# Gate products of the two mixer blocks: two 128-column tiles at a time, as seven half-size block products

## The chip, the cores and the metric

One core of one Trainium2 chip runs the whole program. The metric is the device time of one execution in microseconds, as the median of several runs; less is better. All tensors are float32.

## What is computed

Two blocks of a diffusion-style mixer with expert layers, then one block of a causal mixer. Only the merge of three branches in the first two blocks is touched. Cut to that:

```python
p = h @ w_in[l]          # h: tokens x 1024
g_a, g_b, g_c = jnp.split(jax.nn.sigmoid(p[..., OFF_GATE:]), 3, axis=-1)   # 3 x 1024 wide
merged = g_a * (o_a @ w_branch[0]) + g_b * (o_b @ w_branch[1]) + g_c * (o_c @ w_branch[2])
x = x + gt1 * (merged @ w_out)
```

In the first block (l = 0) there are 768 tokens (512 of x, 256 of the context), in the second (l = 1) 512.

## The kernel before, in words

Activations lie feature-major: `h3[:, k, t]` is feature k*128 + partition of token t, for 8 tiles k. `PLAN[l]` is a list of jobs; every engine walks through the same list in order and does its own part of each job, so the list sets the order of work on all engines (`plan_layer`, L433; the engine programs from L935, L1567, L1645, L1755 on). Two things follow from this: an engine that waits in one job holds back all its later jobs, and what stands in a queue is seen from the list alone.

The part around the change is the dense stage, `conv + gates[2] + gates[0] + gates[1]` (L438 to L440). First come four products `conv_b`, then for each branch (2, 0, 1) and each of eight output tiles d a job `gate` and a job `branch`:

- PE, `gate` (L1083, `product` at L1004): 8 matmuls over k of a 128x128 weight block with all tokens, each split into columns 0 to 511 and 512 to 767 where there are 768 tokens. `branch`: the same with 4 values of k. Each float32 matmul is two instructions in the trace, so a `gate` is 32 instructions in the first block and 16 in the second.
- ScalarE, `gate` (L1906): the sigmoid of the product, PSUM to one of two rows of `probT`.
- VectorE, `branch` (L2287 to L2298): the gate times the branch's product, into `merged`; for branches 0 and 1 a second instruction adds it.

In the first block only, `with_modulation` (L376) spreads 40 jobs `acc` over this list. Each is four VectorE instructions over 1,024 columns that add a 1 MB piece of `w_ada` to running sums in SBUF (L2157, L2159). After four `acc` come the jobs `rsum` (L1134; PE, then a copy on ScalarE) and `adag` (L1143; PE, then VectorE), which turn a finished group into modulation values.

Weights come in chunks through a ring of six SBUF places of 1 MB. A chunk of gate weights is 1024x256, two output tiles. The SP queue issues the loads in the order in which the jobs first need the chunks, and `load` (L1569) waits, before each, until the place's former chunk was used up (`chunk_end`). Since the queue is in order, a load also waits for all loads ahead of it. A chunk of `w_ada` is used up when VectorE has finished its `acc`.

PSUM has eight banks of 512 columns. `begin` (L959) hands three places of two banks each out in turn to the jobs; two single banks, HEAD_SUMS and SIDE, stand beside them. A helper, `Engine.do` (L1725), issues an instruction on VectorE or ScalarE and waits for its end.

## Time and profile before

| what | value |
|---|---|
| median of 3 runs | 3112.27 us |
| lowest, highest | 3110.53, 3115.92 us |
| the profiled execution: its time | 3114.2 us |
| the profiled execution: span, first to last instruction | 3112.4 us |
| mean granted TensorE clock in it | 0.994 |

All durations below come from the profiled execution. Its time stands 1.8 us over its span and 1.9 us over the median of the runs. The page has one row for each engine (busy time), a chain of the work that ended last, and groups of instructions by line. The line numbers are those of the kernel above.

### The profile page before, as it was taken

Reading aid. Unit: us, or ns where it says so; the run is one execution under the profiler, and the core shown is the slowest. Engines: PE = TensorE matmul, PEld = TensorE weight load, DVE = VectorE, ACT = ScalarE, POOL = GpSimd, SP = SyncE. Lnnn points to the kernel's source line nnn. Section 1 sums busy time; section 2 is a strip of 40 time slices with the busy share of each in tenths; the row PEclk is TensorE's granted clock in tenths of the full one; section 3 lists DMA queues with packets and bytes.
Section 4 is the critical chain, followed back from the end, with each engine's and each line's share of the span. In section 5 each row is a group of like instructions: output and inputs, shape, how many; then the busy total and the mean of one; then the engine's idle time right before and its main releaser. Section 6 shows DMA issues by size and latency. Waiting matters only on the chain.

```text
span 3112.4 us, 32607 instructions
## 1 busy us (share of the span) xinstructions
PE 2984.3 (96%) x13043; PEld 1404.1 (45%) x13043; DVE 1052.1 (34%) x1566; ACT 613.1 (20%) x1121; POOL 75.0 (2%) x88
## 2 busy tenths in 40 slices
PE   7999999999999999999999999999979898899999
PEld 4565655555545222222335655444433222234547
DVE  4764645556514000000147554011121010137352
ACT  3135530000003010111031453000011101021161
POOL 1000000000000010101000000000000000000000
PEclk9999999999999999999999999999999999999999
DMA  8120013434413999999870201222489999963200
GB/s 251 41 82 14 15 55 128 176 135 157 161 41 140 397 351 380 355 371 380 298 200 1 68 21 46 68 81 95 162 333 408 408 408 407 408 221 81 68 1 28
DMA packets 266076, 578.83 MB, mean 186 GB/s; under 512 B 62040, under 2 KB 140136, under 8 KB 265800
## 3 DMA queue, kind: packets, MB, share of 16 engines
q1 hardware_dynamic: 258064, 554.09, 48.8%
q0 software_dynamic: 7552, 22.61, 2.4%
q8 instruction: 106, 1.74, 0.2%
q14 instruction: 42, 0.34, 0.0%
q10 hardware_dynamic: 312, 0.05, 0.0%
HBM read 561.49 MB, written 15.20 MB: 185 GB/s over the span
## 4 chain that ended last, share of the span: by engine, by line
PE 84%; DMA 11%; DVE 3%; issue 1%; ACT 1%; SPq 0%; DVEq 0%; POOL 0%; ACTq 0%; POOLq 0%
PE ps L1016 31%; PE ps L1420 9%; PE ps L1535 6%; PE ps L1032 5%; PE ps L1432 5%; PE ps L1080 5%; PE ps L1248 3%; PE ps L1260 3%; PE ps L1294 3%; DMA ring<-in_w_e_up 3%; PE ps L1093 2%; DMA ring<-in_w_e_down 2%; DMA ring<-in_w_e_gate 2%; PE ps L1056 2%; PE ps L1476 2%; PE ps L1230 1%
## 5 line engine op out<-in xcount | busy, mean ns | idle before, releaser
L1016 PE MATMUL ps<-hT,ring 128*128 128x512 f32 (+1 forms) x2080 | 773.2, 529 | 3.0 <-ACT hT L1761 2.9
L1016 PEld LDWEIGHTS ps<-hT,ring 128*128 128x128 f32 x2080 | 394.9, 191 | 367.6 <-issue 343.7
L1420 PE MATMUL ps<-ring,hT 128*64 128x512 f32 x1392 | 333.1, 607 | 17.2 <-DMA ring<-in_w_e_up 11.9
L1420 PEld LDWEIGHTS ps<-ring,hT 128*64 128x64 f32 x1392 | 89.7, 137 | 220.1 <-issue 219.3
L1032 PE MATMUL ps<-hT,ring 128*128 128x512 f32 (+1 forms) x448 | 181.5, 533 | 0.7 <-DVEq L1746 0.7
L1761 ACT ACTIVATE prob<-ps 128x512 f32<-128x512 f32 (+1 forms) x67 | 46.4, 693 | 681.0 <-PE ps L1016 681.0
L1432 PE MATMUL ps<-ring,hT 128*32 128x512 f32 x1392 | 167.4, 598 | 0.5 <-ACT hT L1761 0.5
L1535 PE MATMUL ps<-ring,hT 128*64 128x512 f32 x640 | 150.4, 603 | 15.0 <-DMA ring<-in_w_e_down 10.8
L1761 ACT ACTIVATE prob<-prob,nms 128x768 f32<-128x768 f32 (+5 forms) x224 | 159.2, 711 | 18.9 <-DVE nms L2384 8.6
L1080 PE MATMUL ps<-merged,ring 128*128 128x512 f32 (+1 forms) x384 | 142.7, 526 | 3.1 <-issue 3.1
L1016 PE MATMUL ps<-obuf,ring 128*128 128x512 f32 (+1 forms) x384 | 143.4, 523 | 0.0
L1260 PE MATMUL ps<-con,prob 128*128 128x128 f32 x872 | 140.2, 283 | 1.3 <-DVE merged L2408 0.5
L1260 PEld LDWEIGHTS ps<-con,prob 128*128 128x128 f32 x872 | 96.4, 140 | 89.5 <-issue 78.8
L2534 DVE TENSOR_TENSOR qbuf<-qbuf,ps 128x1536 f32<-128x1536 f32 x8 | 14.0, 1754 | 341.1 <-ACT qbuf L1761 341.1
L1761 ACT ACTIVATE hT<-ps,mod,amp 128x256 f32<-128x256 f32 (+1 forms) x96 | 50.7, 528 | 327.7 <-PE ps L1470 182.1
L2596 DVE SCALAR_TENSOR_TENSOR xT<-ps,mod,xT 128x512 f32<-128x512 f32 x40 | 30.0, 751 | 249.2 <-PE ps L1476 248.8
L1925 ACT COPY merged<-ps 128x512 f32<-128x512 f32 (+1 forms) x128 | 71.5, 559 | 169.9 <-PE ps L1260 129.9
L2296 DVE TENSOR_TENSOR prob<-prob,ps 128x768 f32<-128x768 f32 (+1 forms) x32 | 26.2, 820 | 231.6 <-PE ps L1016 231.6
L1248 PE MATMUL ps<-kbuf,obuf 64*128 64x256 f32 (+2 forms) x576 | 100.9, 464 | 2.5 <-DVEq L1746 2.2
L1080 PEld LDWEIGHTS ps<-merged,ring 128*128 128x128 f32 x384 | 71.2, 190 | 70.5 <-issue 67.4
L1016 PEld LDWEIGHTS ps<-obuf,ring 128*128 128x128 f32 x384 | 72.4, 190 | 66.2 <-issue 63.3
L1294 PE MATMUL ps<-merged,vbuf 128*64 128x256 f32 x736 | 96.7, 390 | 0.9 <-DVE merged L2408 0.9
(333 smaller groups left out, 3029.0 us busy)
## 6 DMA issues: line engine op xcount, KB each, us to landing
ring<-in_w_e_gate SPq DMA_DIRECT2D x95, 1024.0 KB, 12.3
ring<-in_w_e_up SPq DMA_DIRECT2D x83, 1024.0 KB, 9.7
ring<-in_w_e_down SPq DMA_DIRECT2D x76, 1024.0 KB, 9.4
ring<-in_w_in SPq DMA_DIRECT2D x49, 1024.0 KB, 5.3
ring<-in_w_ada SPq DMA_DIRECT2D x48, 1024.0 KB, 7.3
ring<-in_w_e_down SPq DMA_DIRECT2D x32, 512.0 KB, 7.2
ring<-in_w_in SPq DMA_DIRECT2D x48, 256.0 KB, 4.7
merged<-in_w_e_up SPq DMA_DIRECT2D x12, 1024.0 KB, 15.1
```

What stands on the lines that cost most here:

```text
L1016: mm = pe.matmul(ps[:, b + a:b + e], lhs[:, k, :], rhs[:, k, a:e], start=k == 0, stop=k == nk - 1)
L1032: mm = pe.matmul(ps[:, BANK[SIDE]:BANK[SIDE] + hi - lo], ring3(slot)[:, k, m % 2 * P:(m % 2 + 1) * P], h3[:, k, lo:hi], start=k == 0, stop ...
L1056: mm = pe.matmul(ps[:, b:b + CH], o2[:, k, t * P:(t + 1) * P], ring3(slot)[:, k, :], start=k == 0, stop=k == KD - 1)
L1080: mm = pe.matmul(ps[:, b:b + e - a], w[:, k, :], m3[:, k, a:e], start=k == 0, stop=k == KD - 1)
L1248: mm = pe.matmul(ps[:, b[a] + c0:b[a] + c0 + w], q[r, u["g"], u["q0"]:u["q0"] + P], k[r, u["kj"], k0:k0 + w], start=True, stop=True)
L1260: mm = pe.transpose(ps[:, o:o + P], scored(j[1], j[2], a, u)[:, m * P:(m + 1) * P], ident)
L1294: mm = pe.matmul(out_, v(tiles[m], col), exp_, start=m == 0, stop=m == len(tiles) - 1, tile_position=(0, a * HD))
L1420: mm = pe.matmul(ps[e * CX:(e + 1) * CX, b + h * 512:b + (h + 1) * 512], lhs, second_weights(slot_of[sub], e, h), start=k == 0, stop=k == ...
L1432: mm = pe.matmul(ps[q:q + CC, b + 1024:b + 1536], lhs, second_weights(slot_of[k % 2], e, h), start=k == 0, stop=k == KD - 1, tile_position ...
L1535: mm = pe.matmul(to, lhs[:, k, s0:s0 + CX], second_weights(slot, e, h), start=k == 0, stop=k == KD - 1, tile_position=(0, e * CX))
L1761: return sc.activation(o, i, f, **kw)
L1925: A.do(sc.copy(*turned_to(j)), tb_done[r], j)
```

## The change

Two output tiles (256 columns of gate weights, one chunk) become one job `gate2`. The weights are seen as 2x2 blocks (two halves of k, two output tiles), the tokens as 2x2 blocks (two halves of k, two halves of the token columns). Instead of eight block products it makes seven, of 4 values of k with half of the tokens each (384 columns in the first block, 256 in the second), from sums of blocks:

- `hsum`, once in a block, on VectorE: seven instructions that make sums of token blocks. In the first block they lie in ring places 4 and 5, so that the chunks of the dense stage go round the four others.
- `wsum`, once for each pair of tiles, on GpSimd: four instructions of 512 columns that make sums of weight blocks, in one set of buffers. It waits for the chunk and for the last product of the pair before.
- `gate2` on PE: p1; then, after `wsum`, p6 and p5; p7 waits for VectorE's u2, p2 for ScalarE's copy of p1, p4 for u3, p3 for "22". ScalarE copies p1 and takes four sigmoids; VectorE makes five additions. Six of the seven products are thus behind the weight sums.
- The list becomes `gate2`, `branch` 2n, `wsum` of the next pair, `branch` 2n+1. An `acc` stands only behind a `gate2` or an even `branch`; the 12 pairs have 1, 3, 2, 2, 3, 2, 2, 3, 2, 2, 3 and 0 of them behind `gate2` and one each (the last none) behind the even `branch`.

```diff
+        spare = ring[:, RING - 2:RING, :].rearrange("p s f -> p (s f)")
+
+        def four(cols):
+            return cols.rearrange("p (k t) -> p k t", k=4)
+
+        token_sums = [(four(spare[:, 0:2 * NT]), four(spare[:, 2 * NT:4 * NT]),
+                       [spare[:, 4 * NT + k * NT // 2:4 * NT + (k + 1) * NT // 2] for k in range(2)] + [rs[:, 0:NT // 2], rs[:, NT // 2:NT]]),
+                      (h3[:, 0:4, NX:NT], h3[:, 4:8, NX:NT], [m3[:, k, NX:NT] for k in range(4)])]
+        weight_sums = [four(b) for b in (kbuf[:, D:D + 512], vbuf[:, 2 * D:2 * D + 512], pr[:].rearrange("p k t -> p (k t)")[:, D:D + 512])]
...
+            def long(j):
+                return {"hsum": 0, "wsum": 0, "gate2": 2}.get(j[0], 1)
...
-            count, passed, share = len(todo), 0, len(jobs) - 4
+            count, passed, share = len(todo), 0, sum(map(long, jobs)) - 4
             order, due = [], []
             for j in jobs:
                 order.append(j)
-                passed += 1
+                passed += long(j)
                 while due and due[0][0] <= passed:
                     order.append(due.pop(0)[1])
+                if j[0] == "wsum" or j[0] == "branch" and j[3] % 2:
+                    continue
                 while todo and (count - len(todo)) * share < passed * count:
...
-            gates = {br: [(w, l, br, d) for d in range(KD) for w in ("gate", "branch")] for br in range(3)}
-            dense = conv + gates[2] + gates[0] + gates[1]
+            pairs = [(l, br, n) for br in (2, 0, 1) for n in range(KD // 2)]
+            dense = conv + [("hsum", l), ("wsum",) + pairs[0]]
+            for at, (_, br, n) in enumerate(pairs):
+                dense += [("gate2", l, br, n), ("branch", l, br, 2 * n)]
+                dense += [("wsum",) + p for p in pairs[at + 1:at + 2]] + [("branch", l, br, 2 * n + 1)]
...
+                if j == ("hsum", 0):
+                    few[0] = True
+                elif few[0] and j[0] == "wout":
+                    few[0] = False
+                    after_sums.extend((len(chunks), s) for s in (RING - 2, RING - 1))
                 for key in chunk_keys(j):
                     if key not in chunk_key:
-                        add_chunk(key, chunk_dmas(key))
+                        if few[0]:
+                            add_chunk(key, chunk_dmas(key), few[1] % (RING - 2))
+                            few[1] += 1
+                        else:
+                            add_chunk(key, chunk_dmas(key))
...
+            def seven_products(j):
+                l = j[1]
+                half = (NT, NX)[l] // 2
+                cn, slot = weights(chunk_of(j)[0])
+                if j[1:] == PAIRS_FIRST[l]:
+                    need(oT_ready, ("O", l, 2 * TILES[l] - 1))
+                    need(token_sums_ready, ("hsum", l))
+                a = begin(j)
+                b = a + 512
+                third = (HEAD_SUMS, SIDE)[j[3] % 2]
+                c = begin(j + ("c",), third)
+                w = ring3(slot)
+                s1, s2, s4 = weight_sums
+                t1, t2, t4 = token_sums[l]
+                def times(name, bank, lhs, rhs, first):
+                    for k in range(4):
+                        mm = pe.matmul(ps[:, bank:bank + half], lhs[:, k, :], rhs[k] if name == "p4" else rhs[:, k, :],
+                                       start=first and k == 0, stop=k == 3, skip_group_check=not first)
+                    mm.then_inc(seven_full.sem, 1)
+                times("p1", a, w[:, 0:4, 0:P], h3[:, 0:4, 0:half], True)
+                need(weight_sums_ready, ("wsum",) + j[1:])
+                times("p6", b, s2, t2, True)
+                times("p5", c, s1, t1, True)
+                need(seven_added, j[1:] + ("u2",))
+                times("p7", b, w[:, 0:4, P:2 * P], h3[:, 0:4, half:2 * half], False)
+                need(first_product, j[1:])
+                times("p2", a, w[:, 4:8, 0:P], h3[:, 4:8, 0:half], False)
+                need(seven_added, j[1:] + ("u3",))
+                times("p4", b, w[:, 4:8, P:2 * P], t4, False)
+                need(seven_added, j[1:] + ("22",))
+                times("p3", c, s4, h3[:, 4:8, half:2 * half], False)
+                chunk_end[cn] = (seven_full.sem, seven_full.at[j[1:] + ("p3",)])
...
+                for since, place in after_sums:
+                    if n >= since and slot == place and (chunk_prev[n] is None or chunk_prev[n] < since):
+                        sp.wait_ge(seven_full.sem, seven_full.at[LAST_PAIR[0] + ("p3",)])
...
+            def weight_sum(j):
+                slot, value = chunk_at[chunk_key[chunk_of(j)[0]]]
+                pool.wait_ge(w_full[slot], value)
+                if ("gate2",) + j[1:] in gate_before:
+                    pool.wait_ge(seven_full.sem, seven_full.at[gate_before[("gate2",) + j[1:]] + ("p3",)])
+                else:
+                    pool.wait_ge(token_sums_ready.sem, token_sums_ready.at["hsum", j[1]])
+                a = ring3(slot)
+                a11, a12, a21, a22 = a[:, 0:4, 0:P], a[:, 4:8, 0:P], a[:, 0:4, P:2 * P], a[:, 4:8, P:2 * P]
+                s1, s2, s4 = weight_sums
+                added[0] += 2
+                pool.tensor_tensor(s1, a21, a22, ALU.add).then_inc(s_pool_sum, 1)
+                pool.wait_ge(s_pool_sum, added[0] - 1)
+                pool.tensor_tensor(s2, s1, a11, ALU.subtract).then_inc(s_pool_sum, 1)
+                pool.wait_ge(s_pool_sum, added[0])
+                pool.tensor_tensor(s4, a12, s2, ALU.subtract).then_inc(weight_sums_ready.sem, 1)
+                pool.tensor_tensor(a21, a11, a21, ALU.subtract).then_inc(weight_sums_ready.sem, 1)
...
+                elif kind == "gate2":
+                    half = (NT, NX)[l] // 2
+                    b = BANK[job[j][0]]
+                    if j[1:] != PAIRS_FIRST[l]:
+                        A.need(gate_used, branch_before[j])
+                    A.need(seven_full, j[1:] + ("p1",))
+                    A.do(sc.copy(probT[:, 1, 0:half], ps[:, b:b + half]), first_product, j[1:])
+                    A.need(seven_full, j[1:] + ("p2",))
+                    A.do(func(probT[:, 0, 0:half], ps[:, b:b + half], ACT.Sigmoid), pair_sigmoid, j[1:] + ("11",))
+                    for m, n, q in ((1, 1, "22"), (1, 0, "21"), (0, 1, "12")):
+                        A.need(seven_added, j[1:] + (q,))
+                        g = probT[:, m, n * half:(n + 1) * half]
+                        A.do(func(g, g, ACT.Sigmoid), pair_sigmoid, j[1:] + (q,))
...
+                elif kind == "hsum":
+                    half = (NT, NX)[l] // 2
+                    b11, b12 = h3[:, 0:4, 0:half], h3[:, 0:4, half:2 * half]
+                    b21, b22 = h3[:, 4:8, 0:half], h3[:, 4:8, half:2 * half]
+                    t1, t2, t4 = token_sums[l]
+                    V.do(v.tensor_tensor(t1, b12, b11, ALU.subtract))
+                    V.do(v.tensor_tensor(t2, b22, t1, ALU.subtract))
+                    for k in range(4):
+                        V.do(v.tensor_tensor(t4[k], b21[:, k, :], t2[:, k, :], ALU.subtract))
+                    V.do(v.tensor_tensor(b12, b22, b12, ALU.subtract), token_sums_ready, j)
+                elif kind == "gate2":
+                    half = (NT, NX)[l] // 2
+                    b, c = BANK[job[j][0]] + 512, BANK[job[j + ("c",)][0]]
+                    second, third = ps[:, b:b + half], ps[:, c:c + half]
+                    p1, c12, c22 = probT[:, 1, 0:half], probT[:, 0, half:2 * half], probT[:, 1, half:2 * half]
+                    V.need(first_product, j[1:])
+                    V.need(seven_full, j[1:] + ("p6",))
+                    V.do(v.tensor_tensor(c12, p1, second, ALU.add), seven_added, j[1:] + ("u2",))
+                    V.need(seven_full, j[1:] + ("p7",))
+                    V.do(v.tensor_tensor(c22, p1, second, ALU.add), seven_added, j[1:] + ("u3",))
+                    V.do(v.tensor_tensor(c22, c22, third, ALU.add), seven_added, j[1:] + ("22",))
+                    V.need(seven_full, j[1:] + ("p4",))
+                    V.do(v.tensor_tensor(p1, p1, second, ALU.add), seven_added, j[1:] + ("21",))
+                    V.need(pair_sigmoid, j[1:] + ("11",))
+                    V.release(j)
+                    V.need(seven_full, j[1:] + ("p3",))
+                    V.do(v.tensor_tensor(c12, c12, third, ALU.add), seven_added, j[1:] + ("12",))
+                    V.release(j + ("c",))
                 elif kind == "branch":
                     br, d = j[2], j[3]
                     g = probT[:, d % 2, 0:w]
-                    V.need(sig_ready, ("gate", l, br, d))
+                    V.need(pair_sigmoid, (l, br, d // 2, "12"))
```

## Rows read from the trace of the kernel before

**Rows 1.** Page, part 1: engine, busy us (share of span), instructions

```profile
PE 2984.3 (96%) x13043; PEld 1404.1 (45%) x13043; DVE 1052.1 (34%) x1566; ACT 613.1 (20%) x1121; POOL 75.0 (2%) x88
```

**Rows 2.** Page, part 4: shares of the chain that ended last

```profile
PE 84%; DMA 11%; DVE 3%; issue 1%; ACT 1%; SPq 0%; DVEq 0%; POOL 0%; ACTq 0%; POOLq 0%
```

**Rows 3.** Windows: stretch, its length, busy us by engine, clock, DMA share, GB/s

```profile
480.00:872.00 392.00, 391.98 (x1391) 230.70 (x1390) 222.05 (x213) 26.59 (x35) 0.00 (x0) 1.00 0.45 152
...
1920.00:2196.00 276.00, 274.77 (x656) 121.59 (x654) 30.52 (x46) 15.61 (x25) 1.08 (x2) 1.00 0.24 76
```

**Rows 4.** Chain in order of time: start, length, engine, line, instructions

```profile
65.87 10.32 PE ps L1016 x32
...
1621.22 6.87 PE ps L1016 x16
```

**Rows 5.** The same chain at the start of the dense stage, first block

```profile
438.21 56.96 PE ps L1016 x176
495.16 1.00 PE ps L1140 x16
496.17 10.52 PE ps L1016 x32
506.68 0.79 PE ps L1150 x8
507.47 31.07 PE ps L1016 x96
```

**Rows 6.** Instructions in time, PE, where the first block's gates end

```profile
872.34 0.55 PE L1159 MATMUL ps<-mod,wr 128*16 128x2 f32 x16
```

**Rows 7.** VectorE, groups by shape in 480 to 880: busy, mean ns, idle before

```profile
L2159 DVE SCALAR_TENSOR_TENSOR vbuf<-ring,silc,vbuf 128x1024 f32<-128x1024 f32 x60 | 77.1, 1285 | 2.7
...
L2298 DVE TENSOR_TENSOR merged<-merged,prob 128x768 f32<-128x768 f32 x16 | 15.3, 958 | 2.3
...
L2157 DVE TENSOR_SCALAR vbuf<-ring,silc 128x1024 f32<-128x1024 f32 x8 | 6.0, 754 | 0.7 <-DVE merged L2293 0.4
```

**Rows 8.** VectorE, groups by shape in 1915 to 2200

```profile
L2293 DVE TENSOR_TENSOR merged<-prob,ps 128x512 f32<-128x512 f32 x8 | 5.5, 686 | 77.0 <-PE ps L1016 77.0
```

**Rows 9.** VectorE, groups by shape in 2290 to 2780

```profile
L2607 DVE TENSOR_TENSOR qbuf<-qbuf,ps 128x1024 f32<-128x1024 f32 x16 | 19.5, 1221 | 188.5 <-ACT qbuf L1761 106.0 <-PE ps L1535 82.4
```

**Rows 10.** Page, part 5: a VectorE group of 1,536 columns

```profile
L2534 DVE TENSOR_TENSOR qbuf<-qbuf,ps 128x1536 f32<-128x1536 f32 x8 | 14.0, 1754 | 341.1 <-ACT qbuf L1761 341.1
```

**Rows 11.** Instructions in time, VectorE: it empties the last conv_b

```profile
479.79 0.95 DVE L2285 TENSOR_TENSOR qbuf<-qbuf,ps 128x768 f32<-128x768 f32 x1 [3.98 <-PE ps L1016]
```

**Rows 12.** ScalarE, groups by shape in 1000 to 1140

```profile
L1965 ACT COPY hT<-ps 128x384 f32<-128x384 f32 x8 | 3.8, 478 | 47.2 <-PE ps L1329 47.2
```

**Rows 13.** Waits of the SP queue in 440 to 880: us, times, longest

```profile
SPq L1598 <- PE ps L1016: 348.4, 26, 26.5
```

**Rows 14.** DMA issues in 1900 to 2190: KB each, median us to landing

```profile
ring<-in_w_in SPq DMA_DIRECT2D x10, 1024.0 KB, 5.0
ring<-in_w_branch SPq DMA_DIRECT2D x16, 256.0 KB, 3.8
```

**Rows 15.** GpSimd, groups by shape, whole span

```profile
L1684 POOL MEMSET qbuf<- 128x1024 f32 x1 | 1.0, 977 | 0.0
```

**Rows 16.** Instructions in time, GpSimd, back to back

```profile
1132.39 0.93 POOL L1657 DMA_INDIRECT vbuf<-token_rows0x,idx  x1 [118.41 <-PE ps L1317]
1133.62 0.94 POOL L1657 DMA_INDIRECT vbuf<-token_rows0x,idx  x1 [0.30 <-issue]
```

**Rows 17.** Windows around PE's idle time in the second router

```profile
2272.00:2273.00 1.00, 0.00 (x0) 0.00 (x0) 0.97 (x3) 0.00 (x0) 0.00 (x0) 0.58 1.04 426
...
2284.00:2285.00 1.00, 1.00 (x2) 0.34 (x1) 0.00 (x0) 0.00 (x0) 0.70 (x2) 0.50 0.55 70
...
2286.00:2287.00 1.00, 1.00 (x4) 0.44 (x3) 0.00 (x0) 0.00 (x0) 0.00 (x0) 1.00 0.90 344
```

**Rows 18.** Instructions in time, PE, behind that idle time

```profile
2266.35 1.91 PE L1204 MATMUL ps<-con,xT 128*128 128x128 f32 x16
2280.39 1.04 PE L956 MATMUL ps<-of_expert,prob 128*128 128x16 f32 x4 [12.13 <-DVE prob L2457]
2282.34 5.41 PE L950 MATMUL ps<-con 128*128 128x512 f32 x8 [0.91 <-DVEq L1750]
```

More of the change, by code:

```diff
@@ L505, in program @@
         oT_ready = event("outT_ready", of("O"))
-        sig_ready = event("gate_sigmoid", of("gate", "silg"))
+        sig_ready = event("gate_sigmoid", of("silg"))
+        token_sums_ready, weight_sums_ready = event("token_sums_ready", of("hsum")), event("weight_sums_ready", [k for j in of("wsum") for k in (j + (1,), j)])
+        seven_full = event("seven_products_full", [j[1:] + (p,) for j in of("gate2") for p in SEVEN])
+        first_product = event("first_product_copied", [j[1:] for j in of("gate2")])
+        seven_added = event("seven_products_added", [j[1:] + (q,) for j in of("gate2") for q in ("u2", "u3", "22", "21", "12")])
+        pair_sigmoid = event("gate_pair_sigmoid", [j[1:] + (q,) for j in of("gate2") for q in ("11", "22", "21", "12")])
+        PAIRS_FIRST = {l: [j for j in PLAN[l] if j[0] == "gate2"][0][1:] for l in range(DEPTH)}
+        branch_before, gate_before = {}, {}
+        for l in range(DEPTH):
+            dense_jobs = [j for j in PLAN[l] if j[0] in ("gate2", "branch")]
+            gates_in_order = [j for j in dense_jobs if j[0] == "gate2"]
+            gate_before.update({j: i[1:] for i, j in zip(gates_in_order, gates_in_order[1:])})
+            branch_before.update({j: dense_jobs[n - 1] for n, j in enumerate(dense_jobs) if j[0] == "gate2" and n})
+        LAST_PAIR = {l: [j for j in PLAN[l] if j[0] == "gate2"][-1][1:] for l in range(DEPTH)}
         gate_used = event("gate_used", of("branch", "silg"))
@@ L676, in program @@
         chunk_key = {}
+        few, after_sums = [False, 0], []
         def second_place(r):
@@ L780, in chunk_of @@
                 return (kind, l, t // 2), t % 2
-            if kind == "gate":
-                return ("gate", l, t, j[3] // 2), j[3] % 2
+            if kind in ("gate2", "wsum"):
+                return ("gate", l, t, j[3]), 0
             if kind == "branch":
@@ L820, in chunk_dmas @@
             return plain(w_out[l], n * CH)
-        WEIGHTED = ("qk", "v", "conv_c", "conv_x", "conv_b", "gate", "branch", "silg", "side", "wout", "wt")
+        WEIGHTED = ("qk", "v", "conv_c", "conv_x", "conv_b", "gate2", "wsum", "branch", "silg", "side", "wout", "wt")
         def chunk_keys(j):
@@ L1059, in run @@
                     chunk_end[cn] = (full[job[j][0]], job[j][2])
-                elif kind in ("conv_c", "conv_x") or kind == "silg" and j in job:
+                elif kind in ("conv_c", "conv_x", "hsum", "wsum") or kind == "silg" and j in job:
                     pass
-                elif kind in ("qk", "conv_b", "gate", "silg", "branch", "wout"):
+                elif kind == "gate2":
+                    seven_products(j)
+                elif kind in ("qk", "conv_b", "silg", "branch", "wout"):
                     ck, m = chunk_of(j)
@@ L1691, in _ @@
             for l in range(DEPTH):
+                for j in PLAN[l]:
+                    if j[0] == "wsum":
+                        weight_sum(j)
                 if l == 1:
@@ L1894, in run @@
                     token_tile(j)
[L1895 removed]
+                elif kind == "gate2":
[11 more added lines that the diff above has]
+                        A.do(func(g, g, ACT.Sigmoid), pair_sigmoid, j[1:] + (q,))
+                elif kind == "silg":
                     w = width(l, "")
[L1897 removed]
+                    n = j[2]
                     b = A.read(j)
[L1899 to L1910 removed]
+                    if n >= 2:
+                        A.need(gate_used, ("silg", l, n - 1 - (n < 4)))
+                    A.do(func(rs[:, 0:w] if n >= 4 else probT[:, n % 2, 0:w], ps[:, b:b + w], ACT.Tanh, scale=0.5), sig_ready, j)
                 elif kind == "E":
```

17 lines of the change are left out of this document (4 added, 13 removed).

## The prediction

> **What bounds the kernel now.** Look first at the busy times: PE 96% of the span, VectorE 34%, GpSimd 2% [rows 1]. The chain of waits says the same of the path: 84% PE, 11% DMA [rows 2]. Then the stage that is edited, by windows: in 392 us of the first block's gates PE is busy 391.98 us, in 276 us of the second's 274.77, at clock 1.00 in both; VectorE has 222 us in the first, 30.5 in the second [rows 3]. So both stages are PE's, and fewer product columns would shorten them one for one, as long as nothing else gets in front of PE. But the two stages differ: in the first VectorE is half full, and its jobs also set free the ring's places. The SP queue waits 348 us there for PE to use up chunks, up to 26.5 us at a time [rows 13]: with six places the loads are far ahead.
>
> **Products, removed and added.** 16 instructions of 512 columns take 6.87 us, 429.4 ns each; 16 of 512 and 16 of 256 take 10.32 us, so 256 columns take 215.6 ns [rows 4]; 384 lie midway, 322.5 ns. First block, per pair: before 2 x 10.32 = 20.64 us; after 28 products x 2 instructions x 322.5 ns = 18.06; 2.58 less, 31.0 us for 12 pairs. One block product is 2.58 us. Second block: before 2 x 6.87 = 13.74, after 56 x 215.6 ns = 12.07; 1.67 less, 20 us for 12. A block product is 1.73 us. 51 us in all is the most that the change can save; the rest of this part is what eats it.
>
> **Start of each stage.** The token sums can only be made when the last conv_b is done with h3. First block: VectorE starts to empty conv_b 0.3 us behind PE's end (438.21 + 4 x 10.32 = 479.49, VectorE at 479.79, 0.95 us) [rows 5, 11]. Behind it in the list stands an acc, 4 x (1.285 + 0.035 us between two) = 5.3 us [rows 7], then hsum: three instructions of 1,536 columns at 1.754 [rows 10], four of 384 at 0.55 (768 columns take 0.958 [rows 7], 512 0.686 [rows 8]; 1.05 ns a column, so 384 take 0.55), gaps 0.3: 7.8. PE idles 14.3 us; p1 is hidden behind the weight sums. Second block: 0.3 + 0.7 + three of 1,024 at 1.221 [rows 9] + four of 256 at 0.42 + gaps = 6.5 us.
>
> **Weight sums on GpSimd.** The trace has no such instruction. The nearest row is a memset of 1,024 columns, one stream, 977 ns [rows 15]. From below: four of 512 columns at that rate, 0.49 us each, 2.0 us. From above: two streams read and one written, each at the memset's 0.95 ns a column, 1.46 us, and behind each the 0.30 us that lies between two GpSimd instructions [rows 16]: 7.0 us. I take 7.0, since three streams and a wait on its own semaphore stand in the code; 2.0 stays for the range. The Trainium skill (GPSIMD Engine Reference, section 3.1, "Elementwise") has 4497 ns for 2,048 columns, so by that page an estimate of 1.1 us for 512; its sum is the first rival's. In the second block the sums have 2 branches and p1, 6.87 + 1.73 = 8.6 us, and six places in the ring keep the chunk early: hidden, at 1.5 us to spare. So there only the start counts: 6.5 + 7.1 - 1.73 = 11.9 us, and 1.5 us of slow clock (below). Second block: -20 + 13.4 = -6.5 us.
>
> **First block, pair after pair.** Four places hold gate chunk, two or three w_ada chunks and the branch chunk, so the next gate chunk goes where the chunk four loads before lay. With two acc behind gate2 (six of the eleven intervals: G, A, A, B, A, G) that is the first A, and VectorE takes it only behind the pair's last product. From p3 to p3: 0.3 + the last addition 0.6 + acc 5.3 = 6.2; issue 0.1; landing 5.0 [rows 14], 11.3; sums 7.1, 18.5; then six products behind them, 15.5: **34.0 us**. With three (four intervals) the place is the second A's: 5.3 more, **39.3 us**. The interval behind the first pair has its place free at p3 (0 + 5.1 + 7.1 = 12.2, PE needs 14.9): PE's own 10.32 + 2.0 (rsum, adag [rows 5]) + 18.06 = 30.4. Where adag, or rsum and adag, stand between gate2 and the first acc, VectorE first waits for them: 1.0 us in five intervals, 1.9 in three (PE 1.0, ScalarE's copy, PE 0.79 [rows 5]), 10.7. Sum: 30.4 + 6 x 34.0 + 4 x 39.3 + 10.7 = 402. Before the first p3: conv_b 41.3 + 14.3 + 7.1 + 15.5 = 78.2. After the last: 10.3 + rsum, adag and the copy between them, 2.9 = 13.2. **493.7 us** against 872.34 - 438.21 = 434.1 before [rows 5, 6]: +59.6. The path over VectorE alone (two acc, a branch at 1.95, an acc, a branch, ScalarE's copy of 384 at 0.48 [rows 12], u2, four products) is 0.9 + 15.9 + 3.9 + 1.6 + 10.3 = 32.6, close behind: the cover under the weight path is thin. A branch chunk behind three acc waits for its own pair's p3 and lands 4 us late [rows 14]; the weight path hides that.
>
> **Clock.** PE had been idle since 2268.26 when its clock fell, to 0.58 in the window 2272 to 2273, and it was back at 1.00 in 2286 to 2287, 4 us after the work of 2282.34 [rows 17, 18]. Here PE waits some 4 us in ten pairs, and 14 at the start. Between nothing and 2 us each (4 us at half the speed), I take 1: +10 us.
>
> **Sum.** +59.6 + 10 - 6.5 = +63: the profiled execution's 3114.2 becomes 3177; its time is 1.9 over the median, so 3175 for the median. At no cost: ScalarE's copy and four sigmoids (under 3 us of ScalarE in 28), the additions between products (1.3 us under a product of 2.58, 1.1 under 1.73), GpSimd's later constants (needed 600 us later), the expert stages, which only shift.
>
> **Rivals.**
> 1. *Cheap sums.* The four take 5.2 us, not 7.0. Ten intervals and both starts lose 1.8, the clock half of its 10: -27, **3148**. For it: 1.46 puts the three streams one behind another. Against: no row has a two-stream instruction on GpSimd. Sums cheaper still bring little more, since the VectorE path of 32.6 takes over.
> 2. *GpSimd and VectorE get in each other's way.* The sums run just when VectorE works through its acc, each reading ring and running sum from SBUF. If each sum waits for one acc instruction (1.32) and the reverse, four sums of 1.3 take some 9.5 us, not 7.1, and an acc that meets them gets up to 5 us longer, which the weight path mostly covers: +24 in ten intervals, +10 for the clock's full 20 us, -4 at the two starts, where VectorE rests: +30, **3205**. No row shows both at work on SBUF, so nothing here excludes or proves it; the second block hardly has it (two-input instructions 11 us in 276). The Trainium skill (SBUF — State Buffer, section "Who interferes with whom") says that a VectorE instruction with two SBUF inputs and a GpSimd instruction that reads SBUF exclude each other for a whole instruction; by that rule this rival is what comes. No run here shows it.
> 3. *Faster.* The gate chunk lands in time, because its load doesn't wait for an acc. Then every interval is PE's 30.4: 11 x 30.4 + 78.2 + 13.2 = 425.8, -8.3, with -6.5 from the second block: -15, **3097**. It decides at 2.7 us behind p3 (14.9 less 5.1 and 7.1); the first acc ends at 6.2. For it: I may have an order of loads wrong. Against: the first A stands behind gate2 in the list of VectorE, in every pair but the last.
>
> **Chances and range.** Forecast 0.42, rival 2 0.28, rival 1 0.20, rival 3 0.07, and 0.03 for a mix near no change. The range has to take in the forecast, rival 1 with somewhat cheaper sums (3138) and rival 2 to a little beyond its number: 3138 to 3215. A measurement can tell 0.2%, some 6 us. Faster by more: rival 3, 0.07. Within: 0.03. Slower: 0.90.
>
> **What the profile after would show.** Right: PE's seven products at 322 and 216 ns an instruction; PE waiting for GpSimd at p6 in the first block for about 4 us a pair, and 14 us for VectorE once; the load of the next gate chunk issued 6 us (or 11.5) behind p3; the first block's dense stage near 500 us, the second's about 6 us shorter than before, with no waits inside. Wrong: GpSimd's instruction at 1.2 or over 2 us (rivals 1 and 2), acc instructions over 1.29 us where they meet GpSimd's (rival 2), no wait at p6 (rival 3). The forecast fails altogether if the loads don't follow the acc, or if PE doesn't keep its pace at 384 columns.

## The result, and the profile after

The changed kernel takes 3182.04 us, the median of 4 runs (3178.43 to 3184.54), against 3111.40 for the kernel before, also of 4 runs (3109.62 to 3115.92): ratio 1.0225, interval 1.0210 to 1.0241. It is slower, 7 us above the predicted 3175 and inside the range. Its profiled execution took 3178.43 us, the shortest of the four, with a span of 3176.6 us against 3112.4 before; all comparisons of stages below are between profiled executions.

The page of the changed kernel, part 1, then the chain by engine (for [rows 1, 2]):

```profile
PE 2961.6 (93%) x13235; PEld 1449.2 (46%) x13235; DVE 1159.8 (37%) x1700; ACT 634.3 (20%) x1193; POOL 221.4 (7%) x184
...
PE 77%; DMA 12%; DVE 5%; POOL 2%; issue 1%; ACT 1%; SPq 0%; DVEq 0%; ACTq 0%; POOLq 0%
```

On the path VectorE's share has gone from 3% to 5% and GpSimd's from 0% to 2%. To see where the 64.2 us come from (3176.6 less 3112.4), both executions are cut at the same four points: the first conv_b of each block, and the small product behind the last branch (L1159 before, L1241 after). Before, these are 438.21, 872.34, 1919.42 and 2194.21; after, 436.97, 952.20, 1993.70 and 2259.16, so the pieces are: ahead of the stage -1.2, first dense stage 434.1 to 515.2, **+81.1**; between the two 1047.1 to 1041.5, -5.6; second dense stage 274.8 to 265.5, **-9.3**; the rest -0.8. Windows over the two stages after (stretch, its length, busy us by engine with instructions, clock, DMA share, GB/s; for [rows 3]):

```profile
436.97:952.20 515.23, 435.39 (x1425) 247.84 (x1424) 312.51 (x296) 37.60 (x71) 85.45 (x48) 0.92 0.35 117
...
1993.70:2259.16 265.46, 257.30 (x931) 177.15 (x932) 65.08 (x110) 25.38 (x61) 61.91 (x50) 0.99 0.26 79
```

Before, PE's busy time was the whole stage: 434.1 and 274.8 us, at clock 1.00. Now it is 435.4 of 515.2 us at clock 0.92, although the products are 31.0 us cheaper. This gives the split used through the rest: **idle**, the stage less PE's busy time, 515.2 - 435.4 = 79.8 us; **slow clock**, PE's busy time less what its products take at full pace, 435.4 - (434.1 - 31.0) = 32.3 us; products -31.0; sum +81.1. In the second block: idle 8.2, slow clock 257.3 - (274.8 - 20.0) = 2.5, products -20.0.

What PE waited for in the first of them (the list of waits in 430 to 945: engine and line, releaser, us in total, times, longest):

```profile
PE ps L1081 <- POOL ring L1785: 44.8, 10, 5.8
PE ps L1081 <- issue: 14.4, 1, 14.4
PE ps L1059 <- DMA ring<-in_w_branch: 11.1, 4, 3.9
```

L1081 is the products of `gate2`, L1785 the last weight sum, the 14.4 the wait for the token sums at the start; the third line is branch chunks that came late. One pair in the chain in order of time (start, length, what):

```profile
526.60 18.07 PE ps L1081 x56
...
544.70 0.56 DVE prob L2425
...
545.40 1.29 DVE kbuf L2271
...
554.64 1.30 DVE prob L2271
555.94 0.02 issue
555.95 5.20 DMA ring<-in_w_in
...
561.22 1.28 POOL kbuf L1780
...
562.57 2.14 POOL vbuf L1782
...
564.77 2.12 POOL prob L1784
566.89 2.21 POOL ring L1785
...
569.15 18.13 PE ps L1081 x48
```

These are the seven products at full clock, then VectorE's last addition and two `acc` (eight L2271, first and last shown), the load issued 11.3 us behind p3, its landing 5.2 us later, four sums, then p6. The interval from p3 to p3 is 42.6 us. And the last line shows the clock: 48 instructions took 18.13 us where 15.5 would be full pace. Two windows of that stretch:

```profile
564.00:567.00 3.00, 0.11 (x1) 0.00 (x0) 2.96 (x2) 0.00 (x0) 2.92 (x3) 1.00 1.01 414
...
570.00:573.00 3.00, 3.00 (x6) 1.63 (x5) 1.13 (x2) 0.48 (x1) 0.00 (x0) 0.50 0.54 171
```

PE does nothing for some 5 us, and the work behind it runs at granted clock 0.50, the 1.2 GHz level.

The next rows show what is called **the turns** below: while GpSimd's sums and VectorE's `acc` run side by side, both get longer (instructions in time, GpSimd, then VectorE):

```profile
561.22 1.27 POOL L1780 TENSOR_TENSOR kbuf<-ring 128x512 f32<-128x512 f32 x1 [35.56 <-DMA ring<-in_w_in]
562.57 2.13 POOL L1782 TENSOR_TENSOR vbuf<-kbuf,ring 128x512 f32<-128x512 f32 x1
564.77 2.12 POOL L1784 TENSOR_TENSOR prob<-ring,vbuf 128x512 f32<-128x512 f32 x1
566.85 2.24 POOL L1785 TENSOR_TENSOR ring<-ring 128x512 f32<-128x512 f32 x1
```

```profile
554.64 1.28 DVE L2271 SCALAR_TENSOR_TENSOR prob<-ring,silc,prob 128x1024 f32<-128x1024 f32 x1
...
560.18 0.95 DVE L2433 TENSOR_TENSOR merged<-prob,ps 128x768 f32<-128x768 f32 x1
561.28 8.90 DVE L2271 SCALAR_TENSOR_TENSOR vbuf<-ring,silc,vbuf 128x1024 f32<-128x1024 f32 x4
570.21 0.95 DVE L2433 TENSOR_TENSOR merged<-prob,ps 128x768 f32<-128x768 f32 x1
```

The four `acc` instructions from 561.28 take 2.22 us each, against 1.285 alone; the first sum, 1.27, began before them, the others take 2.13, 2.12 and 2.24. The branch instructions, with one of their inputs in PSUM, keep their 0.95. In the second block, where VectorE rests, all four are cheap, and so are all later sums but one (1.81, at 2161.91, beside a branch addition with both inputs in SBUF):

```profile
2027.97 1.26 POOL L1780 TENSOR_TENSOR kbuf<-ring 128x512 f32<-128x512 f32 x1 [495.88 <-DVE hT L2408]
...
2031.87 1.26 POOL L1785 TENSOR_TENSOR ring<-ring 128x512 f32<-128x512 f32 x1
```

So four sums cost 5.2 us alone. In the ten pairs in which PE waits for them they take 6.6 to 8.6 us, 7.6 on average. The forecast of 7.0 lies between.

### The profile page after: what moved, and what is told of

It is laid out like the page before. It is cut to its first block, busy times and chain, and to the rows that moved or that the text cites. A ratio compares the mean times of both kernels' runs of the same rounds, so it can differ in the third digit from the quotient of the medians.

```text
span 3176.6 us, 33439 instructions
## 1 busy us (share of the span) xinstructions
PE 2961.6 (93%) x13235; PEld 1449.2 (46%) x13235; DVE 1159.8 (37%) x1700; ACT 634.3 (20%) x1193; POOL 221.4 (7%) x184
## 4 chain that ended last, share of the span: by engine, by line
PE 77%; DMA 12%; DVE 5%; POOL 2%; issue 1%; ACT 1%; SPq 0%; DVEq 0%; ACTq 0%; POOLq 0%
PE ps L1059 14%; PE ps L1081 11%; PE ps L1502 8%; PE ps L1617 6%; PE ps L1112 5%; PE ps L1162 4%; PE ps L1514 4%; PE ps L1330 3%; PE ps L1342 3%; PE ps L1376 3%; DMA ring<-in_w_e_up 3%; PE ps L1175 2%; DMA ring<-in_w_e_gate 2%; DMA ring<-in_w_e_down 2%; PE ps L1136 2%; PE ps L1558 2%
## 5 line engine op out<-in xcount | busy, mean ns | idle before, releaser
L1059 PE MATMUL ps<-hT,ring 128*128 128x512 f32 (+1 forms) x928 | 351.0, 536 | 2.1 <-ACT hT L1869 2.1
L1059 PEld LDWEIGHTS ps<-hT,ring 128*128 128x128 f32 x928 | 176.4, 191 | 171.0 <-issue 155.6
L1081 PE MATMUL ps<-hT,ring 128*128 128x384 f32 (+1 forms) x576 | 168.3, 443 | 25.6 <-issue 21.1
L1112 PE MATMUL ps<-hT,ring 128*128 128x512 f32 (+1 forms) x448 | 181.5, 533 | 0.7 <-DVEq L1854 0.7
L1617 PE MATMUL ps<-ring,hT 128*64 128x512 f32 x640 | 149.9, 600 | 16.4 <-DMA ring<-in_w_e_down 10.9
L1081 PEld LDWEIGHTS ps<-hT,ring 128*128 128x128 f32 x576 | 110.5, 194 | 79.7 <-issue 30.7
L1780 POOL TENSOR_TENSOR kbuf<-ring 128x512 f32<-128x512 f32 x24 | 31.2, 1300 | 1382.6 <-DVE hT L2408 893.9
L2271 DVE SCALAR_TENSOR_TENSOR vbuf<-ring,silc,vbuf 128x1024 f32<-128x1024 f32 x70 | 103.3, 1476 | 3.2
L1162 PEld LDWEIGHTS ps<-merged,ring 128*128 128x128 f32 x384 | 71.2, 190 | 70.6 <-issue 67.4
```

Of the source, the lines that this page charges most:

```text
L1059: mm = pe.matmul(ps[:, b + a:b + e], lhs[:, k, :], rhs[:, k, a:e], start=k == 0, stop=k == nk - 1)
L1081: mm = pe.matmul(ps[:, bank:bank + half], lhs[:, k, :], rhs[k] if name == "p4" else rhs[:, k, :], start=first and k == 0, stop=k == 3, ski ...
L1112: mm = pe.matmul(ps[:, BANK[SIDE]:BANK[SIDE] + hi - lo], ring3(slot)[:, k, m % 2 * P:(m % 2 + 1) * P], h3[:, k, lo:hi], start=k == 0, stop ...
L1162: mm = pe.matmul(ps[:, b:b + e - a], w[:, k, :], m3[:, k, a:e], start=k == 0, stop=k == KD - 1)
L1617: mm = pe.matmul(to, lhs[:, k, s0:s0 + CX], second_weights(slot, e, h), start=k == 0, stop=k == KD - 1, tile_position=(0, e * CX))
L2271: ins = v.scalar_tensor_tensor(macc[n % 2][w], weight, s, macc[n % 2][w], ALU.mult, ALU.add)
```

## The experiments

Two theories for the first block stand at the start. **Weight path**: each gate chunk is late because it waits for `acc`, lands and is summed, and the turns lengthen both (rival 2). **VectorE's order**: even with the chunk in time, `acc`, branches and additions in one list keep PE waiting for u2 and "22". The table has the first dense stage of every kernel that changes it, split as above (idle from the windows; the last column sums the three, with products at -31.0 except in e8, which keeps the old ones). Of the experiments e1, e2 and e10 have 7, 5 and 4 runs, the others one each.

| kernel | PE idle us | slow clock us | stage against before us |
|---|---|---|---|
| changed kernel | 79.8 | 32.3 | +81.1 |
| e5 no token sums, ring of four | 71.9 | 33.9 | +74.8 |
| e6 no token sums, ring of six | 75.1 | 25.6 | +69.7 |
| e4 GpSimd writes only | 55.2 | 14.4 | +38.6 |
| e3 no weight sums | 48.4 | 19.1 | +36.4 |
| e9 no sums at all, ring of six | 48.9 | 17.8 | +35.7 |
| e10 an `acc` inside each pair | 45.4 | 19.8 | +34.2 |
| e7 `acc` of 32 columns | 31.9 | 13.1 | +14.0 |
| e8 kernel before, ring of four | 35.1 | 15.8 | +50.9 |

**e1_second_only: the seven products only in the second block.** The first block keeps the jobs of before, with six ring places.

```diff
...
-            dense = conv + [("hsum", l), ("wsum",) + pairs[0]]
-            for at, (_, br, n) in enumerate(pairs):
+            dense = conv + (gates[2] + gates[0] + gates[1] if l == 0 else [("hsum", l), ("wsum",) + pairs[0]])
+            for at, (_, br, n) in enumerate(pairs if l else []):
...
```

> Seven products in the second block only; the first block's gates are those of the kernel before. Theory A (the loss is all in the first block, by VectorE's acc jobs, the loads behind them and the sums): the first block's dense stage back from 515.2 to 434 us, the second's stays at 265.5 against 274.8 before, so about 9 us faster than before, 3102. Theory B (the second block gains nothing by itself, its stage only looks shorter because the first shifted it, or the expert stage takes the gain back while it waits for its loads): about 3111.

3101.79 us, ratio 0.9969 (0.9958 to 0.9980): faster than before by 0.3%. The second dense stage is 1916.82 to 2183.88, 267.1 us, against 274.8; from p3 of the first pair on, the chain is PE alone (6.87 for two branches, 12.09 for 56 product instructions). So the loss of the change is all in the first block.

**e2_sums_early: e1, and the sums of the second block ahead of conv_b.** Six of the seven token sums need only what conv_b doesn't write last; the seventh, in place, goes behind it as `hlast`, and only p7 waits for it.

```diff
-            dense = conv + (gates[2] + gates[0] + gates[1] if l == 0 else [("hsum", l), ("wsum",) + pairs[0]])
+            dense = ([("hsum", l), ("wsum",) + (l, 2, 0)] if l else []) + conv + (gates[2] + gates[0] + gates[1] if l == 0 else [("hlast", l)])
...
+                if j[1:] == PAIRS_FIRST[l]:
+                    need(token_sums_ready, ("hlast", l))
                 times("p7", b, w[:, 0:4, P:2 * P], h3[:, 0:4, half:2 * half], False)
```

> As e1, with the second block's token sums and the first weight sums made ahead of the four conv_b products, except the sum that overwrites a block of h, which only p7 waits for. Theory A: the 11.7 us of PE's wait at the start of the dense stage (token sums 6.5, weight sums 5.2) go, and the stage is 4 x 6.87 + 12 x (12.07 + 6.87) = 254.8 us with no wait, 20 us under before: 3091. Rival: VectorE is late behind the end of attention, 6 us more of work there stop conv_b's PSUM places or PE in attention, and half or more of it comes back: 3096 to 3102.

3091.92 us, ratio 0.9935 (0.9922 to 0.9949), the best of all kernels here. Its chain at the start of the second stage, and the window over it:

```profile
1917.21 27.66 PE ps L1060 x64
1944.87 12.09 PE ps L1082 x56
1956.96 6.87 PE ps L1060 x16
```

```profile
1917.21:2172.24 255.03, 255.03 (x928) 176.16 (x929) 65.94 (x110) 25.36 (x61) 61.39 (x50) 1.00 0.27 82
```

There is no idle time, the clock is 1.00, and the stage is 274.8 - 255.0 = 19.8 us shorter than before, nearly all of the 20.0 that the products save. The arithmetic of the change pays where nothing stands in front of PE.

**e3_no_weight_sums: GpSimd makes none**, the products read the chunk's own blocks in their place (the output is then not the reference's).

```diff
-                s1, s2, s4 = weight_sums
+                s1, s2, s4 = w[:, 4:8, P:2 * P], w[:, 0:4, P:2 * P], w[:, 4:8, 0:P]
...
-                pool.tensor_tensor(s1, a21, a22, ALU.add).then_inc(s_pool_sum, 1)
...
+                pool.sem_inc(weight_sums_ready.sem, 2)
```

> The changed kernel without GpSimd's four sums; the products read the chunk's own blocks in place of the sums. The waits for chunk, pair before and the GpSimd semaphore stay. Theory A (the chain p3, VectorE's first acc, the next gate load, the sums, p6): without sums the load is still 11.3 us behind p3 and VectorE's own path of 31 to 39 us an interval is next; first block 25 to 31 us slower than before instead of 81, so about 3125 in all, with VectorE's acc instruction back at 1.285 us. Theory C (the sums and their quarrel with VectorE are the whole loss): PE's own 30.4 us an interval, about 3093.

3137.95 us. The stage is still 36.4 longer than before, 5 more than the upper end expected. The long `acc` instructions all take 1.285 us. PE's waits in the pairs now name VectorE:

```profile
PE ps L1081 <- issue: 14.4, 1, 14.4
PE ps L1081 <- DVE prob L2410: 13.5, 7, 2.8
PE ps L1059 <- DMA ring<-in_w_branch: 11.0, 4, 3.9
```

and the chain goes through VectorE from one p3 to the next u2 (L2265 `acc`, L2430 and L2432 branch, L2410 u2, L2419 the last addition, "12"):

```profile
648.50 1.30 DVE vbuf L2265
...
661.71 0.96 DVE prob L2430
...
662.80 0.97 DVE merged L2432
663.80 1.30 DVE vbuf L2265
...
671.17 0.49 ACT prob L2003
671.69 0.04 issue
671.74 0.56 DVE prob L2410
672.35 12.30 PE ps L1081 x32
684.66 0.57 DVE prob L2419
```

That is the "path over VectorE alone" of the prediction, here with rsum, adag and three `acc` behind p3: 41.3 us from one last addition (643.39) to the next. In it 32 product instructions take 12.30 us, 2.0 over full pace.

**e4_writes_only: GpSimd busy as before, but it reads nothing**: eight memsets of 512 columns in place of four sums (output not the reference's).

```diff
...
+                for n, to in enumerate((s1, s1, s2, s2, s4, s4)):
+                    pool.memset(to, 0.0).then_inc(s_pool_sum, 1)
+                    pool.wait_ge(s_pool_sum, added[0] - 5 + n)
+                pool.memset(s4, 0.0).then_inc(weight_sums_ready.sem, 1)
+                pool.memset(s2, 0.0).then_inc(weight_sums_ready.sem, 1)
```

> The changed kernel with GpSimd's four sums replaced by eight memsets of 512 columns, 0.5 us each, each behind the one before: about the same 5 us of GpSimd, but with no SBUF input; the products use what the memsets left. Theory D (a GpSimd instruction that reads SBUF and a VectorE instruction with two SBUF inputs take turns): the eight stay at 5 us in every pair, acc instructions stay at 1.285 us, the wait at p6 falls from 4.2 us a pair to about 1.5, first block 36 to 40 us slower than before instead of 81: about 3140. Rival (any GpSimd instruction slows VectorE, or the DMA traffic does it): acc instructions still at 2.2 us, about 3180.

3137.51 us, the stage +38.6. The memsets take 0.52 us each (median), 4.5 us a pair, also beside `acc`, and `acc` keeps its 1.285. PE's longest group of waits:

```profile
PE ps L1081 <- POOL vbuf L1784: 15.3, 10, 1.7
```

The fill is about 0.7 us a pair shorter than four resting sums (5.2), the reads are gone, and the stage is 42.5 us shorter than the changed kernel's: 24.6 of idle and 17.9 of clock. Ten pairs at 0.7 are 7, so the turns cost some 35 to 42 us. The clock's part can be seen at p6: behind each of e4's ten waits there, 1.0 to 1.7 us long, the first 8 instructions take 2.85 us, full pace. Without the turns GpSimd costs the stage little: e4 has 6.8 us more idle than e3 and 4.7 less slow clock, 2 us more in all.

**e10_acc_inside: one of the `acc` behind each pair moved between the pair's additions**, two instructions behind u2, two behind "22"; with the same work in all.

```diff
                     V.do(v.tensor_tensor(c12, p1, second, ALU.add), seven_added, j[1:] + ("u2",))
+                    steps = acc_steps(inside[j]) if j in inside else iter(())
+                    next(steps, None)
+                    next(steps, None)
...
                     V.do(v.tensor_tensor(c22, c22, third, ALU.add), seven_added, j[1:] + ("22",))
+                    for _ in steps:
+                        pass
```

> The changed kernel, all sums kept, with one thing moved on VectorE: the first acc behind each gate2 is done inside it, two of its instructions behind u2 and two behind the addition 22, while PE is in p7, p2 and p4. Theory A (the interval is VectorE's own order of work and the load behind the first acc): each of the ten long intervals loses one acc, 5.3 us, from both paths, and the next gate load is free by p3; by the same step-by-step working, with the turns of GpSimd and VectorE in it, the first block's dense stage is 32 to 39 us over before instead of 81: about 3137. Rival (the four ring places or the quarrel over SBUF set the interval, whatever the order): under 15 us gained, above 3167.

3138.94 us, ratio 1.0085 (1.0068 to 1.0101), near the 3137 expected. With turns and ring of four left as they are, the stage is 46.9 shorter: VectorE now works while PE makes the products. The wait for GpSimd falls from 44.8 to 15.5 us.

**e6_six_places: no token sums, so the dense stage's loads go round six places.** The products read token blocks instead (output not the reference's).

```diff
-                if j == ("hsum", 0):
+                if False:
                     few[0] = True
```

> The changed kernel without token sums (the products read the blocks of h themselves), so that all six ring places stay in use in the first block; the weight sums are kept. Theory A1 (the late load of the next gate chunk is what costs): chunk and branch chunk are early, PE's own 30.4 us an interval, first block about 18 us under before: near 3078. Theory A2 (VectorE's acc in front of the branch and of u2, made longer by the turns with GpSimd, costs the most, and the late load lies under it): first block still 55 to 70 us over before, second 15 under: near 3158.

3164.05 us, near the second theory's 3158. The next run, **e5_no_token_sums**, is its partner, the same without token sums but with four places, so that the two differ in the ring alone.

```diff
...
-                    V.do(v.tensor_tensor(t1, b12, b11, ALU.subtract))
...
+                    dve.sem_inc(token_sums_ready.sem, 1)
```

> The changed kernel without the token sums (the products read the blocks of h themselves); four ring places and the weight sums are kept, so it is to e6 as four places are to six. Theory A: only VectorE's 7.8 us at the start of the first block's dense stage and 5.6 us at the second's go, 13 us: about 3169, with ten long intervals as in the changed kernel, and e6 stands 5 to 11 us under it. Rival (the token sums cost more than their start, since they also fill what PE reads): under 3155.

3171.26 us, as expected. PE's longest groups of waits, first in e6, then in e5:

```profile
PE ps L1082 <- DVE prob L2413: 38.3, 5, 11.8
PE ps L1082 <- issue: 16.6, 4, 6.7
```

```profile
PE ps L1082 <- POOL ring L1786: 46.4, 11, 5.9
PE ps L1082 <- issue: 6.7, 1, 6.7
```

With six places the chunks are in time, GpSimd is off the path (0.7 us left), and PE waits as long, for VectorE's u2. Two places more give 5.1 us. The token sums at the start cost 6.3 us (e5 against the changed kernel; idle at the start 6.7 in place of 14.4).

**e9_six_no_sums: e6 without the weight sums too**, so neither a late chunk nor a turn nor a sum is left; what stays of the change is the seven products, their additions and copies, and the order of the list.

> As e6, six ring places and no token sums, and without the weight sums too: of the change only the seven products, their additions and copies and the list order are left. Theory A2 (VectorE's order, an acc of 5.3 us between a product and the branch or u2 behind it, costs by itself): the first block's dense stage still 17 to 29 us over before, the second's 20 under: 3110 to 3120. Rival (with ring and sums out of the way nothing is left but the products): the first block 31 under, the second 20: about 3061.

Its diff is that of e3 and e6 together. 3128.58 us, missing the expected 3110 to 3120; the stage is +35.7, nearly e3's +36.4, which has the token sums and four places. Idle 48.9 us, mostly for VectorE:

```profile
PE ps L1082 <- DVE prob L2407: 26.6, 7, 8.2
PE ps L1082 <- issue: 15.2, 3, 6.7
```

So VectorE's list, with the additions that PE waits for, costs by itself more than the products save. Which part of that is the order, this run doesn't separate; e10, the same work in another order, gives 46.9 us of it back, with the sums in place. The expectation left out the clock, here 17.8 us.

**e7_short_acc: `acc` on 32 columns of 1,024** (all its `scalar_tensor_tensor` instructions; the modulation values are then wrong in the other columns), which empties VectorE with loads, order and sums in place.

```diff
-                            ins = v.scalar_tensor_tensor(macc[n % 2][w], weight, s, macc[n % 2][w], ALU.mult, ALU.add)
+                            ins = v.scalar_tensor_tensor(part, weight[:, 0:32], s, part, ALU.mult, ALU.add)
```

> The changed kernel with the scalar_tensor_tensor instructions of the acc jobs cut to 32 of 1,024 columns; loads, waits and all else stay. Theory A (VectorE's acc is the cause behind load, order and quarrel alike): sums back at 5.1 us, first block 1 us under to 4 us over before, only the branch chunks that wait for their own pair's last product still late, 4 us in four pairs: about 3103. Rival (the ring of four or PE's own waits between products cost by themselves): above 3125.

3115.17 us, 12 above what was expected. The stage is 67 us shorter than the changed kernel's, and +14.0 against before. What is left: 10.3 us at the start, 10.9 for branch chunks, 7.3 for GpSimd, 3.5 for `adag`, and 13.1 of slow clock, which again was not in the expectation. The four waits make up the 31.9 of idle.

**e8_before_four: the kernel before, its first dense stage with four ring places.** No product, sum or order is changed.

```diff
...
+                if j == ("gate", 0, 2, 0):
+                    few[0] = True
+                elif j[0] == "wout":
+                    few[0] = False
...
+                            add_chunk(key, chunk_dmas(key), few[1] % (RING - 2))
```

> The kernel before with one change: in the first block's dense stage its chunks go round four ring places in place of six. If four places are too few for the loads between VectorE's acc jobs, as the step-by-step working gives for it: 30 to 39 us slower than before, about 3145. Rival (the loads are far ahead, the SP queue waits 348 us there, so two places can be spared): within 5 us of 3111.

3163.44 us, 52 above the kernel before; the larger expectation was 30 to 39. The first line is PE's wait for gate chunks; the second the window over the stage:

```profile
PE ps L1025 <- DMA ring<-in_w_in: 35.1, 11, 6.1
```

```profile
437.19:922.23 485.04, 449.95 (x1521) 260.20 (x1521) 240.16 (x229) 26.61 (x35) 0.00 (x0) 0.96 0.38 124
```

That is 35.1 us of waiting and 449.9 - 434.1 = 15.8 of slow clock. In the old order two ring places are worth 50.9 us, although the SP queue waits 348 us there for PE [rows 13]. In the new order, where VectorE's path lies just beneath, they are worth 5 us with the weight sums (e5, e6), and without them 0.7 together with the token sums (e3, e9).

## Why the prediction was right

The number was right in part by luck. The weight path stood as forecast, but the forecast priced the sums, alone, too high (7.0 for 5.2) and left out the turns that made them 7.6 on average in the ten long pairs; the two nearly cancel. What was wrong beyond that is the clock. The parts one by one:

**Products.** 322.5 and 215.6 ns an instruction held: 56 take 18.07 us in the first block (forecast 18.06) and 12.09 in the second (12.07). e2 gives 19.8 of the 20.0 us back in full.

**Start of each stage.** 14.3 us forecast, 14.4 measured, in the first block. In the second, 11.9 of idle and 1.5 of clock were forecast, 13.4 together; measured are 8.2 and 2.5, together 10.7, and 1.8 of the difference is the sums at 5.2 us. At both starts p1 ran at half pace (8 instructions in 5.46 and 3.66 us) in time in which PE would have waited for the sums, so part of the forecast idle is booked as slow clock.

**Weight sums.** Mis-sized as a price: 7.0 taken, 5.2 measured where GpSimd is alone, 7.6 on average in the ten long pairs. That 7.0 comes near the 7.6 is luck: the working has three streams one behind another, the trace has a shorter instruction made longer by turns. The bound from the memset's rate, one stream behind another (1.46 an instruction), was too high against 1.27, and the 0.30 between two instructions [rows 16] is 0.08 here. The Trainium skill (GPSIMD Engine Reference, section 3.1, "Elementwise") gives by its figure for 2,048 columns an estimate of 1.1; the trace has 1.27. In the second block this is rival 1's price (the prediction gives no working for its 5.2), and 1.8 of the 2.8 us by which the stage came out under the forecast (-9.3 for -6.5).

**Rival 2** was real, and the forecast had left it out. Its price was 24 us of waiting in ten intervals and 10 of clock; e4 against the changed kernel gives 24.6 of waiting (up to 7 of them the shorter fill) and 17.9 of clock. The Trainium skill (SBUF — State Buffer, section "Who interferes with whom") says that a VectorE instruction with two SBUF inputs contends with a GpSimd instruction that reads SBUF, not with one that only writes it; the trace agrees on who meets whom: 2.12 to 2.24 against 1.27 and 2.22 against 1.285 for readers, no change beside `acc` for e4's memsets (0.52 us), or beside the sums for the branch instructions with an input in PSUM (0.95). It doesn't agree that one shuts the other out for a whole instruction, as the prediction read it: 1.27 and 1.285 make 2.55, and each took under 2.25.

**The intervals.** From the first p3 to the last the forecast had 402 us for the eleven, without clock; measured are 424.7 (514.19 to 938.93), 29 of them slow clock. The stage's idle was forecast at 90.6 (59.6 + 31.0) and is 79.8, 11 less in spite of the turns, 4.4 of it at the start (18.8 forecast, with p1 taken off, 14.4 measured). The sequence of the weight path is what the chain shows, piece by piece: the loads follow `acc` and land in 5.2, and p6 waits 4.5 us on average in ten pairs, where the forecast had "some 4 us in ten pairs". The branch chunks' waits (11.1 us, four times, longest 3.9) were to be hidden behind the weight path. They are: they stand ahead of p1, where PE would wait for the sums anyway. "Close behind", the 32.6 of the VectorE path, is the sentence that carried most: e3, e6 and e9 take parts of the weight path away, and in each PE then waits for VectorE's u2. With three `acc` behind p3 it is 41.3 us in e3, against 42.6 for the weight path in the changed kernel; the prediction worked out the case of two alone.

**Clock.** This is the step that failed. 10 us in the first block were forecast, 1 for each wait, from the range "between nothing and 2"; measured are 32.3. The ten waits at p6 and the one at the start were counted rightly. Behind eight of the ten the granted clock fell to 0.50, the 1.2 GHz level, and the 48 instructions behind took 17.3 to 18.2 us in place of 15.5: 18.1 us in all, 1.9 to 2.7 each. The start cost 3.3. The forecast counted no clock for the branch chunks' waits, and behind three of the four (1.7 to 4.0 us long) the two branches took 13.1 to 13.5 us in place of 10.6: 8.0 us more. The remaining 2.9 us are not assigned. Not all of this is a loss: the chain of what ended last goes from p3 over `acc`, load and sums (once over VectorE's branches) to p6 and past the branch products, so the 8.0, and 2.7 of the start in p1, fall in time in which PE would have waited. These 10.7 us are about what the idle time was over-priced by. What counts is the clock behind p6: 18.1 us in ten pairs where the forecast had some 10. The rows at hand [rows 17, 18] had a single fall, behind 12 us of rest. Every kernel of the table shows it, e8 with the old products too: 13 to 34 us of slow clock where PE idles 32 to 80. So here a microsecond of waiting, in pieces of a few, cost 1.3 to 1.5.

In sum: forecast idle 90.6, clock 10 and products -31.0 give +69.6; measured 79.8, 32.3 and -31.0 give +81.1; the second block is -9.3 for -6.5. The errors of 11 and 22 have opposite signs, and 11 of each is the same time booked twice, as said above. Of the 11.5 left over, some 8 are the clock behind p6. The second block takes back 2.8 and the stretch between the two stages, expert work with no edit in it, 5.6, so that the profiled executions differ by 64.2 where 63 was forecast; the medians differ by 70.6. That stretch took 1043 to 1049 us in the profiled executions of the nine experiments that leave its work alone (by the same cuts; 1045.1 in e1, 1048.9 in e10), so some 5 us are within the scatter of one execution; and this one was the shortest of the changed kernel's four, 3.6 us under their median.

**What stays open.** e7, e4, e3 and e10 each change one thing, and their gains don't add: 67 us by short `acc`, 42.5 by writes for reads, 44.7 by no weight sums, 46.9 by the order, where 81.1 + 31.0 is all that there was to gain. The paths overlap, so only "with the others left in" can be said of each. A first block that keeps the gain was not found: e10 is nearest among those that compute the whole. Why the clock falls behind one wait and not behind another (3.0, 3.7 and 3.5 us ended at 606.15, 804.46 and 548.19 without a fall, 2.7 us at 839.22 with one) is open too.

## What to carry to other kernels

Fewer columns on the bounding engine are worth their arithmetic only in a stage with nothing in front of it: the same edit gave 19.8 us in the second block, once its sums were made ahead of the stage, and cost 81 in the first. Before adding a step between a load and its use, follow three things behind one another: which job frees the load's place, what the helper engine meets while it works, and how long the in-order list of the other engine is from result to result; e8 shows that two ring places alone can be worth 50 us. And a wait of PE costs more than its length where the clock falls behind it, in this kernel 1.3 to 1.5 times.

## What the runs showed of the hardware beyond this

- A short `acc` instruction can wait for about a whole sum: in e7 those of 32 columns take 0.25 us alone (540.51) and 1.31 beside a sum of 1.27 (583.05).
- A VectorE instruction with one tensor input gets in GpSimd's way too, and there writes are not spared: in e4 `tensor_scalar` over 1,024 columns took 0.93 and 0.97 us in place of 0.75 (595.19, 596.15), and two memsets beside it 0.95 in place of 0.52.
- All seven waits at p6 of 4.8 to 5.8 us had the granted clock at 0.50 behind them. Shorter ones differ: at 840 to 844, behind a wait of 2.68 us, it fell as well, where it had stayed at 1.00 behind the 3.0 us that ended at 606; behind e4's ten waits of 1.0 to 1.7 us at p6 it never fell:

```profile
840.00:842.00 2.00, 2.00 (x5) 1.16 (x4) 1.93 (x3) 0.00 (x0) 0.00 (x0) 0.55 0.03 10
```
